# Two blocks of a transformer on one core: the shifted bias in four pieces, and first units that multiply the high parts of h first

## The reference

```python
def first_block(x, mem, rel_bias_table, ...):
    h = rmsnorm(x, g[0])
    y = hybrid_mixer(h, rel_bias_table, w_in, w_out, ...)     # z = h @ w_in; attention, gating, rwkv; @ w_out
    x = x + rmsnorm(y, g[1])
    h = rmsnorm(x, g[2])
    y = memory_cross_attention(h, rmsnorm(mem, mem_src_gain), mem_wq, mem_wkv, mem_wo)
    x = x + rmsnorm(y, g[3])
    h = rmsnorm(x, g[4])
    return x + rmsnorm(conv_ffn(h, ffn_w_up, ...), g[5])

# inside the attention of the mixer
bias = jnp.transpose(rel_bias_table[bucket], (2, 0, 1))       # bucket: of the distance
scores = einsum(qb, kw) * dh ** -0.5
scores = where(valid, scores + bias, NEG_INF)

# second_block, twice: h = rmsnorm(x); proj = h @ w_in_2[l]; ...; x = x + y @ w_out_2[l]
```

## Time and profile before

| | |
|---|---|
| median of 3 runs | 2354.45 us (2353.87 to 2355.01) |
| the profiled execution | 2355.84 us |
| its span, first to last instruction | 2354.1 us |
| TensorE, VectorE, ScalarE, GpSimd busy | 96%, 58%, 45%, 3% of the span |
| mean granted clock of TensorE | 0.979 |
| the longest single wait of TensorE | 9.40 us |

### The profile page before, as it was taken

The page is one execution under the profiler, slowest core; times in us unless marked ns, Lnnn a source line. Parts: engine busy times, 40 slices in busy tenths (PEclk is TensorE's granted clock), DMA queues, the critical chain, the costliest instruction groups (busy, mean ns, idle before and its releaser), DMA issues.

```text
span 2354.1 us, 31707 instructions
## 1 busy us (share of the span) xinstructions
PE 2253.3 (96%) x12978; PEld 1959.9 (83%) x12978; DVE 1362.3 (58%) x1718; ACT 1067.9 (45%) x1376; POOL 62.9 (3%) x66
## 2 busy tenths in 40 slices
PE   8799999888989999999999999999999999999998
PEld 7788898787877888888888888888986889889776
DVE  5446666566556666767666444655445555544554
ACT  5343542424455544544555334545435443544443
POOL 0000101002000000000000000000000000000000
PEclk9899999899989999999999999999999999999999
DMA  7756440014634555555565555553550556445143
GB/s 279 189 191 202 163 158 1 1 32 154 203 118 134 190 185 188 186 187 187 186 206 191 190 192 196 185 195 120 181 178 19 180 178 222 159 152 174 59 129 140
DMA packets 237804, 375.59 MB, mean 160 GB/s; under 512 B 8535, under 2 KB 110072, under 8 KB 236920
## 3 DMA queue, kind: packets, MB, share of 16 engines
q1 hardware_dynamic: 229596, 362.83, 46.3%
q10 hardware_dynamic: 8092, 11.11, 1.9%
HBM read 369.45 MB, written 4.46 MB: 159 GB/s over the span
## 4 chain that ended last, share of the span: by engine, by line
PE 65%; issue 5%; DVE 4%; ACT 2%; POOL 0%; DVEq 0%; POOLq 0%; ACTq 0%
PE PS L482 16%; PE PS L441 12%; PE PS L443 12%; PE PS L442 12%; PE PS L485 8%; DVE w_lo L359 1%; PE PS L2062 1%; ACT w_hi L354 1%; PE PS L2152 1%; PE PS L2136 1%; PE PS L2046 1%; PE PS L2827 1%; DVE h_both L938 0%; PE PS L921 0%; ACT spare L2074 0%
## 5 line engine op out<-in xcount | busy, mean ns | idle before, releaser
L359 DVE TENSOR_TENSOR w_lo<-raw,w_hi 128x2048 fp32r<-128x2048 f32 (+2 forms) x340 | 766.8, 2256 | 765.2 <-ACT w_hi L354 765.0
L354 ACT ACTIVATE w_hi<-raw 128x2048 fp32r<-128x2048 f32 (+2 forms) x340 | 641.2, 1886 | 876.0 <-PE PS L443 494.4
L482 PE MATMUL PS<-h_both,w_hi 128*128 128x512 f32 x1968 | 541.6, 397 | 12.2 <-DVE w_lo L359 9.4
L441 PE MATMUL PS<-w_hi,h_both 128*128 128x512 f32 (+2 forms) x1344 | 514.9, 383 | 11.7 <-DVE h_both L943 4.5
L442 PE MATMUL PS<-w_lo,h_both 128*128 128x512 f32 (+2 forms) x1344 | 507.2, 377 | 0.0
L443 PE MATMUL PS<-w_hi,h_both 128*128 128x512 f32 (+2 forms) x1088 | 408.3, 375 | 0.0
L482 PEld LDWEIGHTS PS<-h_both,w_hi 128*128 128x128 f32 x1968 | 338.1, 190 | 59.4 <-ACT arena L609 9.6
L485 PEld LDWEIGHTS PS<-h_both,w_lo 128*128 128x128 f32 x1968 | 303.2, 189 | 42.2
L485 PE MATMUL PS<-h_both,w_lo 128*128 128x256 f32 x1968 | 314.0, 281 | 0.0
L441 PEld LDWEIGHTS PS<-w_hi,h_both 128*128 128x128 f32 x1344 | 254.3, 189 | 60.0 <-issue 6.0
L442 PEld LDWEIGHTS PS<-w_lo,h_both 128*128 128x128 f32 x1344 | 254.6, 189 | 45.4
(11 more groups left out here) (569 smaller groups left out, 2003.4 us busy)
## 6 DMA issues: line engine op xcount, KB each, us to landing
raw<-in_w_in SPq DMA_DIRECT2D x132, 1024.0 KB, 5.0
raw<-in_ffn_w_up SPq DMA_DIRECT2D x176, 512.0 KB, 4.3
raw<-in_w_out SPq DMA_DIRECT2D x48, 1024.0 KB, 5.1
raw<-in_ffn_w_down SPq DMA_DIRECT2D x44, 1024.0 KB, 5.0
raw<-in_mem_wkv SPq DMA_DIRECT2D x8, 1024.0 KB, 11.5
raw<-in_mem_wq SPq DMA_DIRECT2D x4, 1024.0 KB, 5.1
raw<-in_mem_wo SPq DMA_DIRECT2D x4, 1024.0 KB, 7.2
raw<-in_w_in SPq DMA_DIRECT2D x4, 768.0 KB, 4.6
```

The source lines that it names most:

```text
L354: act.activation(w_hi[:, slot % 2, :st.n], raw[:, slot, :st.n], ACT.Copy).then_inc(hi_made, 1)
L359: dve.tensor_tensor(w_lo[:, slot % 2, :st.n], raw[:, slot, :st.n], w_hi[:, slot % 2, :st.n].bitcast(F32), ALU.subtract).then_inc(lo_made, 1)
L441: pe.matmul(ps, l_hi, r_hi, start=start, stop=False, skip_group_check=skip)
L482: pe.matmul(sums, wh[:, k, cs], h_both[:, :, kk, :], start=kk == 0, stop=False, skip_group_check=True)
```

## The change

First, the write of the shifted bias is issued in four pieces of three heads each during ST_C, one behind every third unit, beginning behind the split of the first; ScalarE waits for all four only behind ST_CE. The read back is issued in four pieces as well, as steps of the fill of ST_VB and ST_B1, two units apart. VectorE's wait for it in the mixer counts to 64.

Second, opening_tensor has a new form for unit 0, used in all openings but that of ST_MEM_K: TensorE turns pairs 0 and 1 only, and multiplies block k by its high part as soon as hi(k) is there; behind blocks 0 and 1 it turns pairs 2 and 3; then it multiplies the low parts. Where unit 0 has been split ahead, unscaled_opening_scalar and unscaled_opening_vector split unit 1 ahead of pairs 2 and 3 and not behind them. The opening of ST_BC has its own functions for ScalarE and VectorE, which keep their order.

```diff
+        def multiply_highs_first(pe, q, hi_ready, lo_ready, turn):
+            ...
+            pe.wait_ge(lo_made, q.unit(1))
+            ...
+            for k in range(st.kb):
+                hi_ready(k)
+                for o, ts, ns, first in rows:
+                    pe.matmul(o, h_hi[:, k, ts], wh[:, k, ns], start=k == 0 and first, stop=False, skip_group_check=True)
+                    pe.matmul(o, h_hi[:, k, ts], wl[:, k, ns], start=False, stop=False, skip_group_check=True)
+                for o, _, cs, first in blocks:
+                    pe.matmul(o, wh[:, k, cs], h_hi[:, k, :], start=k == 0 and first, stop=False, skip_group_check=True)
+                    pe.matmul(o, wl[:, k, cs], h_hi[:, k, :], start=False, stop=False, skip_group_check=True)
+                turn(k)
+            for k in range(st.kb):
+                lo_ready(k)
+                for o, ts, ns, _ in rows:
+                    last = pe.matmul(o, h_lo[:, k, ts], wh[:, k, ns], start=False, stop=False, skip_group_check=True)
+                for _, o, cs, _ in blocks:
+                    last = pe.matmul(o, wh[:, k, cs], h_lo[:, k, :], start=False, stop=False, skip_group_check=True)
+            last.then_inc(unit_used, 1)
...
-        def opening_tensor(pe, st, j, block, ready=None):
-            for n in range(4):
+        def opening_tensor(pe, st, j, block, ready=None, highs_first=True):
+            for n in range(2):
                 turn_pair_tensor(pe, j, n, block, ready)
-            for u in range(4):
-                pe.wait_ge(j.dve, j[f"lo{4 * u + 3 if j.single else 2 * u + 1}"])
+            if highs_first:
+                multiply_highs_first(pe, Group(st, 0), lambda k: pe.wait_ge(j.act, j[f"hi{k}"]),
+                                     lambda k: pe.wait_ge(j.dve, j[f"lo{k}"]),
+                                     lambda k: turn_pair_tensor(pe, j, k + 2, block, ready) if k < 2 else None)
+            else:
+                for n in (2, 3):
+                    turn_pair_tensor(pe, j, n, block, ready)
+                pe.wait_ge(j.dve, j["lo3"])
+                multiply(pe, Group(st, 0), 0)
+            yield
+            for n in (4, 5):
+                turn_pair_tensor(pe, j, n, block, ready)
+            for u in range(1, 4):
+                pe.wait_ge(j.dve, j[f"lo{4 * u + 3}"])
                 multiply(pe, Group(st, 0), u)
                 yield
...
             if not made:
                 split_hi(act, Group(st, 0), 0)
+            else:
+                split_hi(act, Group(st, 0), 1)
             for n in range(2, 4):
                 turn_pair_scalar(act, j, n, gain)
             yield
             for u in range(1, 4):
-                split_hi(act, Group(st, 0), u)
+                if u > 1 or not made:
+                    split_hi(act, Group(st, 0), u)
...
             next(quarters, None)
+            if made:
+                split_lo(dve, Group(st, 0), 1)
             for n in range(2, 4):
                 turn_pair_vector(dve, j, n, gain)
...
+        def bias_out(act):
+            for n in range(4):
+                hs = slice(3 * n, 3 * n + 3)
+                act.dma_start(shifted[hs], arena[hs, WROW:WROW + 384].unsqueeze(1).to_broadcast([3, P, 384]))\
+                   .then_inc(rel_out, 16)
+                yield
+                yield
+                yield
+
+        def bias_back(act):
+            for n in range(4):
+                act.dma_start(rel_bias[:, 3 * n:3 * n + 3, :],
+                              bass.AP(shifted.tensor, 3 * n * 384 * P + P - 1, [[383, P], [384 * P, 3], [1, S]]))\
+                   .then_inc(rel_back, 16)
+                yield
+                yield
...
-            act.dma_start(shifted, arena[0:A_H, WROW:WROW + 384].unsqueeze(1).to_broadcast([A_H, P, 384])).then_inc(rel_out, 16)
             run(products_scalar(act, ST_BC, more=True, opening=opening_scalar(act, ST_BC, t_x, gain_of("g_mix"))))
-            act.wait_ge(rel_out, 16)
-            act.dma_start(rel_bias, bass.AP(shifted.tensor, P - 1, [[383, P], [384 * P, A_H], [1, S]])).then_inc(rel_back, 16)
-            run(products_scalar(act, ST_C, before=end_of(ST_BC), more=True))
+            weave(products_scalar(act, ST_C, before=end_of(ST_BC), more=True), bias_out(act))
             run(products_scalar(act, ST_CE, before=end_of(ST_C), more=True))
-            act.wait_ge(rel_back, 16)
+            act.wait_ge(rel_out, 64)
...
-            fill = together(prepare_scalar(act), after(4, gating_scalar(act)), after(4, opened_scalar(act)))
+            fill = together(prepare_scalar(act), after(4, gating_scalar(act)), after(4, opened_scalar(act)), bias_back(act))
```

More of the change, by code:

```diff
@@ L496, in multiply @@
             last.then_inc(unit_used, 1)
+        def multiply_highs_first(pe, q, hi_ready, lo_ready, turn):
+            st, bank, slot = q.st, (2 * q.parity, 2 * q.parity + 1), q.first % 2
+            if st.G + q.c >= 2:
+                late = 0 if st.wide == 0 else -1
+                pe.wait_ge(act_evac, q.number(late))
+                pe.wait_ge(dve_evac, q.number(late))
+            pe.wait_ge(lo_made, q.unit(1))
+            wh = w_hi[:, slot, :st.n].rearrange("p (k n) -> p k n", k=st.kb)
+            wl = w_lo[:, slot, :st.n].rearrange("p (k n) -> p k n", k=st.kb)
+            at_once = bool(st.tok and st.ch)
+            rows, blocks = [], []
+            if st.tok:
+                c0, n = st.tok
+                rows = [(PS[:, bank[1], t * n:(t + 1) * n] if at_once else PS[:, bank[t], :n], slice(t * P, (t + 1) * P),
+                         slice(c0, c0 + n), not (at_once and t)) for t in range(TB)]
+            if st.ch:
+                c0, n = st.ch
+                for c in range(n // P):
+                    cs = slice(c0 + c * P, c0 + (c + 1) * P)
+                    if st.wide is None:
+                        o = PS[:, bank[c // 2], (c % 2) * S:(c % 2 + 1) * S]
+                        blocks.append((o, o, cs, c % 2 == 0))
+                    else:
+                        blocks.append((PS[:, q.bank + c, 0:S], PS[:, q.bank + c, S:2 * S], cs, True))
+            for k in range(st.kb):
[14 more added lines that the diff above has]
+            last.then_inc(unit_used, 1)
@@ L1015, in unscaled_opening_vector @@
             for u in range(1, 4):
-                split_lo(dve, Group(st, 0), u)
+                if u > 1 or not made:
+                    split_lo(dve, Group(st, 0), u)
                 if u < 3:
@@ L1844, in dilated_vector @@
             if h < 2:
-                dve.wait_ge(rel_back, 16)
+                dve.wait_ge(rel_back, 64)
             for t_, (o, n) in enumerate(DILATED):
@@ L3214, in _ @@
             pe.wait_ge(ident_in, 16)
-            run(products_tensor(pe, ST_MEM_K, opening_tensor(pe, ST_MEM_K, t_mem, blocks_of(mem_rows), mem_ready)))
+            run(products_tensor(pe, ST_MEM_K, opening_tensor(pe, ST_MEM_K, t_mem, blocks_of(mem_rows), mem_ready, False)))
             scale_row_tensor(pe, n_mem, MEM_BANK)
```

## The result

The changed kernel takes 2335.44 us (median, 2334.08 to 2336.25); the kernel before took 2354.16 us beside it on the same chip. The ratio is 0.9922 with an interval of 0.9905 to 0.994. The profiled execution took 2335.94 us with a span of 2334.2 us, 19.9 us less than the 2354.1 us of before, where the working had 8.2 us.

What follows compares the result with a forecast made beforehand. PE is busy 2253.3 of 2354.1 us, so only some 100 us of standing or lowered clock can be won. Terms: -12.5 - 4.2 + 8.5 = -8.2 us, from 2354.45 to 2346.2 us, range 2336.5 to 2358.

Steps and rivals of the forecast that it cites:

- Part 1: Between ST_BC and ST_C, the bias no longer waited for: 9.4 us of standing and 3.1 of clock, 12.5 us won.
- Part 2: In ST_C, the write's four pieces delay weight loads: 5.6 us stop plus 2.9 us clock, 8.5 us lost, between 0 and 55.
- the worst is the fourth: it starts at 3 + 3T, its load is through at 3 + 3.92T: In ST_C, pieces over 16.8 us queue up; the load behind the fourth misses 74.4, a stop of 3.92T - 71.4 us.
- T: How long one piece of the write in ST_C lasts: bounds 7.9 and 31.4 us, the middle 19.65 us taken.
- Three engines: In ST_C, a piece of three heads sits on three of the 16 engines, while every load needs all 16.
- the deadline: In ST_C, PE notices a late load only after 24.0 us from unit 0's split; for the fourth piece's load, 74.4 us.
- the rule for one load: In ST_C, a load is shut out for 86/128 of a piece, then alternates: through 0.92 T behind the piece's start.
- The forecast's own formula: PE's stop in ST_C is 3.92T - 71.4 us, nothing below T = 18.2, plus 2.9 us for the clock afterwards.
- Rival (a): In ST_C, pieces stay under 18.2 us, no load is late, all of 16.7 us is won: 2337.8 us; chance 0.3.
- Part 3: In five openings, all but ST_MEM_K's, PE starts behind hi0 and multiplies highs first: 4.2 us won, between -0.5 and 5.
- the wait of 9.4 us: Sign: PE's wait of 9.4 us for w_lo, between ST_BC and ST_C, is gone.
- a wait for w_lo in the last groups of ST_C: Sign: PE waits for w_lo in ST_C's last two groups or ST_CE; if it has none there, rival (a) holds.

Runs made afterwards that it cites:

- bias_only: The kernel before with the bias change alone, openings as before: 2340.37 us, ratio 0.9954.
- apart: The changed kernel with the write's pieces issued behind units 0, 5, 10 and 15, in the order 1, 4, 2, 3: 2336.67 us.
- whole_write: The changed kernel with the write in one DMA of 12 heads behind unit 0 of ST_C, still waited for late: 2342.98 us, ratio 0.9956.
- one_port: The changed kernel with all four pieces read from source partitions 0 to 2, issued as before: 2348.65 us, ratio 0.9982.
- after_more: The changed kernel once more, unchanged, timed beside other runs on one chip: 2334.63 us, ratio 0.9925.
- before_again: The kernel before once more, unchanged, for where its clock falls: 2351.45 us.

## Why the prediction was wrong

**Part 1 was right.** 12.5 us forecast, 12.4 in the profile after, 12.1 in bias_only.

**Part 2 was the term that failed: +8.5 us where it is 0.** The step is "the worst is the fourth: it starts at 3 + 3T, its load is through at 3 + 3.92T". The mean length of a piece was well taken: four pieces leave between 90.2 and 168.2, 19.5 us each against 19.65. (Singly, by apart, they are of two kinds, 23 to 24 and 16 us.) Three engines was right, and so was the deadline (4.0 us late gave 4.3 us of stop in whole_write). Even the rule for one load was fair: 28 us said and 23.7 measured there, 19.1 behind piece 1. What was wrong was to apply it to each piece of a queue that never empties. On the forecast's count, which starts with the split at 86.1, piece 4 starts at 60.0; with its length of 23.8 us the rule lets the load through at 81.9, 7.5 us behind the deadline of 74.4. Measured, the load with that deadline (issued at 141.0) is there at 64.8, and the next two land after 10.4 and 12.3 us, each over 7 us ahead of theirs. The rows it was read from the earlier trace rows show one write that starts on idle engines, and the experiments keep the two cases apart: apart, with a pause, repeats the long landing; the changed kernel, without one, doesn't. Behind a standing backlog the loads go on getting their turns, and a rate, 96 of the write's packets for each load, tells whether PE stops: one load in 4.3 us in 110:150 of the changed kernel, under the 5.61 that a unit takes, and one in 6.2 us in one_port (by the landings it is one in 4.6 and one in 6.9 us). The forecast's own formula gives 5.0 + 2.9 us at T = 19.5 and 22.7 + 2.9 at T = 24; measured are 0 and 10.5 us of stops. The rate is not all of it: in one_port some of the long landing does return with each piece, since loads arrive there 8.4, 6.1 and 4.9 us apart, and then again 8.3. In the changed kernel it does so at piece 4 alone, which has one way out: 6.2 and 7.5 us apart, where 4.6 was usual. Why a backlog helps, and why only in part, stays open: no run shows the order in which an engine takes packets from the two queues.

Rival (a), no stop and 2337.8 us, had 0.3. Its condition, T under 18.2, was not met, on the mean or by the fourth piece; its number came out by luck, not by its mechanism.

**Part 3 was right in its steps.** Compared where the clock falls as often (from the end of the wait for x, at the second q stage of the stop before it, to the first stop over 0.8 us behind the opening): ST_MEM_Q 30.5 us before and 30.2 in after_more, two falls in each (0.15 forecast); first q 192.4 in bias_only and 192.2 in after_more, one fall in each (0.3); second q 297.0 and 296.0 (1.2). ST_UP wins 0.6 in the first profile (0.6 forecast); up to the first q stage it is 1.6 in after_more, but 1.1 of these lie behind the opening, where the kernels don't differ. ST_BC wins 2.0 (1.9), for the reason given: the clock stays up at 68:70. Not seen in the forecast: without part 1 most of these 2.0 us are lost again. Of the 5.9 us that the profile shows for the openings, the 1.7 above the forecast are falls of the clock, two in before's first profile where before_again has one, at ST_MEM_Q and at the first q stage.

**The rest of the miss is clock.** 1.5 us at the second kv stage come with the openings (ten profiles against four) and were not looked for: a stop of 1.8 us that is followed by a fall before is not after. Why is not shown. 1.5 us at the first, and 1.7 at the openings, are differences between executions. Against them stand the 0.3 and 1.2 us that the profile after gave back. So 8.5 (part 2) + 3.0 (kv) + 1.7 (openings) - 0.1 (part 1) - 1.5 = 11.6, of the 11.7 us between 8.2 and 19.9. By the timed runs, 18.7 us instead of 8.2, 8.5 of the 10.5 us are part 2.

**Of what would show it:** the wait of 9.4 us and ScalarE's of 13.5 are gone, as said; q10 alone holds 2.7 engines, as said; a wait for w_lo in the last groups of ST_C, which was to tell the forecast from (a), is absent. The second q stage starts sooner, its wait for lo3 of 1.31 us having become one of 0.22 us for hi0. ST_MEM_Q hardly does.

## What to carry to other kernels

When a long transfer shares engines with a stream of loads, work out two things apart: what the first load behind it has to wait (a latency, paid once for each start on idle engines, against the slack of the buffers) and how often a load gets through afterwards (a rate, against what the consumer uses). Cut into pieces on few engines, one queued behind the other, 2304 KB hide behind work that one undivided write stops for 4 us. With the source of a piece on partitions four apart, it is out in 8 us instead of 24. A clock that falls behind short stops moves the time by 1.7 us at each of them from execution to execution: look at two profiles of the same kernel before giving such a difference to a change.

## What the runs showed of the hardware

- A DMA from three partitions goes at 24 GB/s when they are 0 to 2, at 36 GB/s when they are 3 to 5 or 6 to 8, and at 75 GB/s when they are four apart, on about three engines each time where that was read (2.7 and 3.1); its packets take 171 ns in the first case and 65 ns in the last.
- A write of 12 partitions that starts on idle engines holds a load of all 16 for 23.7 us of its own 31; one of partitions 0 to 2, 23 us long, holds it for 19.1. A piece queued behind another did so much less: loads landed 4.6 us apart behind pieces 2 and 3 of the changed kernel, up to 7.5 behind its piece 4, and up to 8.4 in one_port.
- The same kernel's clock falls in different places from one execution to the next, in steps of 1.7 us each; 17 executions of the kernel before on one chip spread from 2349.27 to 2356.13 us, 19 on another from 2346.05 to 2359.11.
